# Layer two's third projection begun ahead of the context's norm in bank G0, and the decay logarithms of four token tiles one projection later

## What is computed

```python
h_lat = modulate(rmsnorm(x, g_mix_pre[i]), ...)
h_ctx = modulate(rmsnorm(xc, g_mix_pre[i]), ...)
p = h @ w_in
k, v, lr_f, lr_b = jnp.split(p_state, STATE_SPLITS, axis=-1)
logg_f = jax.nn.log_sigmoid((lr_f @ w_dec_f + b_dec_f)) / GLA_TAU
logg_b = jax.nn.log_sigmoid((lr_b @ w_dec_b + b_dec_b)) / GLA_TAU
```

## Time and profile before

| | |
|---|---|
| median of 3 runs | 1609.02 us (1607.54 to 1609.69) |
| the profiled execution, its own time | 1608.07 us |
| its span, first to last instruction | 1606.3 us |
| mean granted TensorE clock in the span | 0.988 of full speed |
| busy: PE, VectorE, ScalarE, POOL | 1542.8, 861.7, 568.2, 592.9 us |

### The profile page before, as it was taken

The page is one execution under the profiler, slowest core; times in us unless marked ns, Lnnn a source line. Parts: engine busy times, 40 slices in busy tenths (PEclk is TensorE's granted clock), DMA queues, the critical chain, the costliest instruction groups (busy, mean ns, idle before and its releaser), DMA issues.

```text
span 1606.3 us, 22916 instructions
## 1 busy us (share of the span) xinstructions
PE 1542.8 (96%) x9056; PEld 1388.5 (86%) x9056; DVE 861.7 (54%) x1316; ACT 568.2 (35%) x916; POOL 592.9 (37%) x309
## 2 busy tenths in 40 slices
PE   5999999999999999999999989999999999999997
PEld 2899999886899999999998769888898888888887
DVE  1576888536756326661465675477656332322237
ACT  4644214425444214441243255432525321231221
POOL 0532211245325524653255223332152544444441
PEclk9999999999999999999999999999999999999999
DMA  9544431355322212222122341653040333322321
GB/s 370 199 166 153 160 123 62 113 172 206 118 63 70 79 37 95 74 72 66 53 80 91 119 158 53 209 198 105 28 158 27 107 106 128 128 94 92 104 82 63
DMA packets 54062, 183.93 MB, mean 115 GB/s; under 512 B 5650, under 2 KB 10642, under 8 KB 51028
## 3 DMA queue, kind: packets, MB, share of 16 engines
q1 hardware_dynamic: 47826, 168.85, 30.9%
q10 hardware_dynamic: 6146, 13.83, 2.5%
HBM read 171.13 MB, written 11.53 MB: 114 GB/s over the span
## 4 chain that ended last, share of the span: by engine, by line
PE 89%; DVE 3%; ACT 3%; DMA 2%; POOL 1%; issue 1%; SPq 1%; DVEq 0%; ACTq 0%; POOLq 0%
PE A L1022 61%; PE A L1274 8%; PE N L1274 4%; PE G L1274 4%; PE G L1329 1%; PE A L1208 1%; PE A L1202 1%; PE G L1177 1%; DMA raw<-modw 1%; PE G L1136 1%; DMA raw<-stream 1%; PE A L1170 1%; PE N L1190 1%; PE A L1216 1%; PE N L1120 1%
## 5 line engine op out<-in xcount | busy, mean ns | idle before, releaser
L960 POOL TENSOR_TENSOR w_lo<-raw,w_hi 128x1024 fp32r<-128x1024 f32 (+2 forms) x163 | 385.7, 2368 | 659.7 <-ACT w_hi L1356 622.5
L1022 PE MATMUL A<-h_hi,w_hi 128*128 128x512 f32 (+2 forms) x1264 | 416.3, 360 | 22.5 <-POOL h_lo L1005 10.4
L1022 PE MATMUL A<-h_hi,w_lo 128*128 128x512 f32 (+2 forms) x1264 | 406.2, 352 | 0.0
L1022 PE MATMUL A<-h_lo,w_hi 128*128 128x512 f32 (+2 forms) x1264 | 406.0, 352 | 0.0
L1356 ACT ACTIVATE w_hi<-raw 128x1024 fp32r<-128x1024 f32 (+2 forms) x163 | 167.3, 1028 | 379.2 <-PE A L1022 336.0
L1022 PEld LDWEIGHTS A<-h_hi,w_hi 128*128 128x128 f32 x1264 | 237.1, 192 | 66.1 <-POOL h_lo L1005 16.2
L1022 PEld LDWEIGHTS A<-h_hi,w_lo 128*128 128x128 f32 x1264 | 239.0, 192 | 22.0
L1022 PEld LDWEIGHTS A<-h_lo,w_hi 128*128 128x128 f32 x1264 | 239.4, 192 | 21.1 <-issue 0.5
L1022 PE MATMUL A<-g_hi,w_hi 128*128 128x384 f32 (+2 forms) x480 | 146.2, 347 | 3.8 <-DVE g_lo L1847 2.0
L1022 PE MATMUL A<-g_lo,w_hi 128*128 128x384 f32 (+2 forms) x480 | 145.2, 345 | 0.0
L1022 PE MATMUL A<-g_hi,w_lo 128*128 128x384 f32 (+2 forms) x480 | 145.0, 345 | 0.0
(11 more groups left out here) (313 smaller groups left out, 2648.2 us busy)
## 6 DMA issues: line engine op xcount, KB each, us to landing
raw<-stream SPq DMA_DIRECT2D x150, 512.0 KB, 3.7
mraw<-modv SPq DMA_DIRECT2D x54, 512.0 KB, 4.3
mraw<-modw SPq DMA_DIRECT2D x10, 1024.0 KB, 6.4
raw<-pairs SPq DMA_DIRECT2D x18, 512.0 KB, 4.8
raw<-modw SPq DMA_DIRECT2D x6, 1024.0 KB, 14.7
x<-x_keep ACTq DMA_DIRECT2D x4, 1536.0 KB, 13.5
raw<-stream SPq DMA_DIRECT2D x16, 384.0 KB, 3.1
bg<-modv SPq DMA_DIRECT2D x10, 512.0 KB, 4.1
```

The source lines that it names most:

```text
L960: pool.tensor_tensor(lo, like_chunk(n, raw[:, n % RAW, 0:WIDTH[n]]), hi.bitcast(F32), ALU.subtract).then_inc(lo_done, 1)
L1022: m = pe.matmul(dst[:, at:at + t1 - t0], a, b[:, k, t0:t1], start=(first and p == 0), stop=(last and p == 2))
```

## The change

Six edits belong together.

1. In the hand-over to layer two, three entries `pre` do the latent half of projection 2 (512 columns) into G0, for the feature tiles 0 and 1, 2 to 4, and 5 to 7 (`PRE`). The first stands ahead of the eight `sq` entries, the second behind the fourth, the third behind the eighth, ahead of the norm.
2. Projection 2 of layer two then does the context's 256 columns alone.
3. ScalarE copies the latent half from G0 to `kT` behind its copies of lr, and the context half from the A bank in the place of the old copy.
4. In layer two the three pairs of `z` stand behind projections 1, 3 and 4, not 1, 2 and 3. Layer one keeps its order.
5. Layer two's z begin with G1, not with G0.
6. Layer two's dot products move by one projection (5 to 19, not 4 to 18).

```diff
--- before.py
+++ after.py
@@ -20,6 +20,7 @@
 HEADS, DK, DV, RANK, CHUNK = 4, 64, 128, 16, 64
 HID = 2816 // P
 BLOCKS = (8, 8, 6)
+PRE = ((0, 2), (2, 5), (5, KT))
 EPS = 1e-6
 LN_SET = "natural_log_exp_and_others"
 
@@ -43,7 +44,7 @@
 
 GROUPS, MW = 3, 2048
 DOTS = {0: dict([(x, 3) for x in range(4, 6)] + [(x, 2) for x in range(6, 19)]),
-        1: dict([(x, 2) for x in range(4, 13)] + [(x, 1) for x in range(13, 19)])}
+        1: dict([(x, 2) for x in range(5, 14)] + [(x, 1) for x in range(14, 20)])}
 FFN_DOTS = {("ffn_in", 0): 3, ("ffn_out", 0): 3, ("ffn_in", 1): 2}
 SLOTS = 3
 X_PIECES = 2
@@ -173,8 +174,14 @@
             piece(6)
             steps("res", 1, range(KT))
             order.append(("head", L, w, 1, 0))
-            steps("sq", 1, range(KT))
             if w:
+                order.append(("pre", L + 1, 0))
+            steps("sq", 1, range(4))
+            if w:
+                order.append(("pre", L + 1, 1))
+            steps("sq", 1, range(4, KT))
+            if w:
+                order.append(("pre", L + 1, 2))
                 order.append(("keep", 1, 1))
             order.append(("rstd",) + nxt + (1,))
             steps("nrm", 1, range(KT))
@@ -232,7 +239,7 @@
         m = list(range(2 * KT, 6 * KT))
         for x, (name, j, _) in enumerate(W_IN):
             order.append(("proj", L, x))
-            if 1 <= x <= 3:
+            if x in ((1, 3, 4) if L else (1, 2, 3)):
                 order.append(("z", L, z.pop(0)))
                 order.append(("z", L, z.pop(0)))
             if 4 <= x <= 9:
@@ -355,7 +362,7 @@
 
 
 FOUR_UNITS = ("N1", "N0", "G0", "G1")
-FULL = ("z", "turn", "suffix", "dstate", "four", "gate", "score", "o", "msq", "mean")
+FULL = ("pre", "z", "turn", "suffix", "dstate", "four", "gate", "score", "o", "msq", "mean")
 
 
 class Plan:
@@ -384,8 +391,10 @@
                 elif kind == "four":
                     units = [FOUR_UNITS[tiles_of(L).index(e[2]) % 4]]
                 else:
-                    units = [f"G{g % 2}"]
+                    units = [f"G{(g + L) % 2}"]
                     g += 1
+            elif kind == "pre" and e[2] == 0:
+                units = ["G0"]
             elif kind == "suffix":
                 units = ["N1"]
             elif kind == "dstate":
@@ -1068,7 +1077,16 @@
                         continue
                     unit_free(e)
                     lo_wait(pe, n0)
-                    project(A[PLAN.acc[e]], n0, in_banks(tokens(L, name)), H).then_inc(chunk_used, 1)
+                    ranges = [(SEQ, TOK, SEQ)] if e[1:] == (1, 2) else in_banks(tokens(L, name))
+                    project(A[PLAN.acc[e]], n0, ranges, H).then_inc(chunk_used, 1)
+                elif kind == "pre":
+                    n, ks = PLAN.n0[("proj", L, 2)], range(*PRE[e[2]])
+                    unit_free(e)
+                    lo_wait(pe, n)
+                    for k in ks:
+                        h_wait(pe, L, 0, 0, k)
+                        m = split_matmul(G[0], n, [(0, SEQ, 0)], k, H, k == 0, k == KT - 1)
+                    m.then_inc(full["pre"], 1)
                 elif kind == "head":
                     w, j, s = e[2:]
                     to = ("ffn_in", L, 0, 0) if w == 0 else ("proj", L + 1, j)
@@ -1476,13 +1494,18 @@
                         half = lambda t, r: t[64 * r:64 * r + 32, 0:T].rearrange("p (a c t) -> p c a t", c=2, t=P)[:, r, :, :]
                         act.activation(half(lrT, 0), half(src, 0), ACT.Copy)
                         act.activation(half(lrT, 1), half(src, 1), ACT.Copy).then_inc(free[f"A{PLAN.acc[e]}"], 1)
+                        if L:
+                            act.wait_ge(full["pre"], len(PRE))
+                            act.activation(kT[:, 1, 0:SEQ], G[0][:, 0:SEQ], ACT.Copy).then_inc(free["G0"], 1)
                         high(n0 + RING)
                         act.preload_act_table_set(LN_SET)
                         continue
                     dst = {"k": kT[:, j % 2, 0:T], "v": (vst if j < 2 else cgz)[:, j % 2, 0:T], "q": qT[:, j % 2, 0:T],
                            "f": uF[:, j % 2, 0:T], "c": cgz[:, j % 2, 0:T], "b": bg[:, j % 2, 0:T], "r": r_s[:, j, 0:T]}[name]
                     src = src[:, 0:T]
-                    if e[2] > 1:
+                    if e[1:] == (1, 2):
+                        dst, src = kT[:, 1, SEQ:TOK], A[PLAN.acc[e]][:, SEQ:TOK]
+                    elif e[2] > 1:
                         dst, src = by_bank(dst, T), out_banks(PLAN.acc[e], T)
                     if name == "r":
                         m = act.activation(dst, src, ACT.Silu)
```

## The result

The changed kernel takes 1617.62 us (median of 5 runs, 1615.02 to 1619.65); the kernel before took 1608.97 us beside it. The ratio is 1.0055 (95% interval 1.0044 to 1.0067): slower by 8.65 us, where +7.46 was forecast and the range reached from 1612.5 to 1620.0. The profiled execution took 1619.65 us, the longest of the five, in a span of 1617.9.

What follows compares the result with a forecast made beforehand. TensorE (PE) was taken as the bound, busy 1542.8 us and 89% of the last chain. 3.54 - 5.58 + 7.00 + 2.5 = +7.46 us on 1609.02 gave 1616.5 us, range 1612.5 to 1620.0.

Steps and rivals of the forecast that it cites:

- The forecast's own range: 1615.4 to 1617.9 us, from slow clock of 1.6 to 3.35 us and 0.2 us on the wait at the transposes.
- norm delayed by 15 matmuls: Hand-over to layer two: six matmuls ahead of the first sum and nine after the fourth delay the context's norm, +3.54 us.
- projection 2 shrinks: Layer two's third projection: 8.53 us of matmuls become 2.95 us in the old place, -5.58 us.
- pause at the transposes: Ahead of the kT transposes: PE stands until VectorE has last read both z results of the last pair, +7.00 us.
- slow clock behind it: On the transposes and projection 5: PE runs at 1.2 GHz after the long pause, +2.5 us, between 1.6 and 3.35.
- slow clock under the context heads: Context heads after the norm: no loss to the lower clock in the forecast, 1.7 us in the rival with chance 0.16.
- rival 1: Context heads also run at the slower clock, costing 1.7 us more: +9.2 us, 1618.2 us; chance 0.16.
- the likeliest case: The forecast itself: +7.46 us, 1616.5 us, with the pause ahead of the kT transposes; chance 0.62.
- rival 2: Filling the norm's pause removes a slow stretch under the context heads, giving back 1.9 us: +5.6 us, 1614.6; chance 0.10.
- the wait at 966.95: Kernel before, context head: PE waited for POOL's low parts until 966.95, so the slow stretch there was taken to cost nothing.
- Part one's gain: Matmuls moved ahead in the hand-over: 3.54 - 5.58 = -2.04 us, so projection 3 begins earlier.
- Rivals 3, 4 and 5: Short wait at transposes, 1607.0 us (0.04); moved work held up, 1618.5 (0.03); half the pause given back, 1613.0 (0.05).

Runs made afterwards that it cites:

- both measurements: The changed kernel, unedited, measured twice: first 1617.62 us, ratio 1.0055, then again beside later runs 1613.70 us, ratio 1.0035.
- the last z in N: The changed kernel with layer two's last two z (token tiles 4 and 5) in banks N0 and N1: 1606.27 us, ratio 0.9984; measured again 1607.03 us.
- the z alone: The kernel before with only layer two's z behind projections 1, 3 and 4 and dot products one projection later: 1617.76 us, ratio 1.0054.

## Why the prediction was right

The direction, the place and the main term held; the range from 1612.5 to 1620.0 took in both measurements. The forecast's own range, 1615.4 to 1617.9, took in the first, 1617.62, and not the second, 1613.70. That +7.46 lies so near the first, +8.65, is in part luck: in its trace two misses offset each other, too much slow clock behind the pause and none under the context heads. Step by step (the first measurement's profile, then the second's):

| step | forecast, us | measured, us | from |
|---|---|---|---|
| norm delayed by 15 matmuls | +3.54 | +3.43, +3.46 | the Ln above; first part's start to first z, 954.98 to 974.85, against 16.41 |
| projection 2 shrinks | -5.58 | -5.67 | first to third pair 19.19 less one pair, 1.06, against 12.46 |
| pause at the transposes | +7.00 | +6.91, +6.92 | the rows above |
| slow clock behind it | +2.5 | +1.35, +1.58 | 10.42 and 10.65 to the next transposes, against 9.07 with the last z in N |
| slow clock under the context heads | 0 (rival 1: 1.7) | +2.1, 0 | 20.62 and 18.51, first sum to first z |
| sum | +7.46 | +8.2, +6.3 | the whole stretch, 62.50 and 60.63 against 54.11: +8.4, +6.5 |

- **The pause** was the likeliest case's core, and the runs bear out its reason: it goes when the banks of the pair change, stays when the parts move, and comes alone with the z.
- **The slow clock behind the pause** was taken too large. The middle of the rows' stretches was taken, 5 us at the lower clock; here it was 2.9 and 3.2 us from the start of the transposes. With the z alone more was lost, 2.0 us by the 11.02 to the next transposes. Why these stretches were shorter than the longer ones of the earlier trace rows stays open; waits inside those do not explain it, since PE is busy for all of the 5.95 us one. The Trainium skill (TensorE: Matmul & The Clock Gate, "Why this matters for your kernels") has pauses send the clock back, and the traces agree at this place in every profile that has the pause: the clock stood at 0.50 to 0.53 behind it in all four.
- **The context heads** were given no slow clock in the forecast, and 0.16 in rival 1. The case was not an either-or: it happens in some executions of one program and not in others. That fits two medians, 1617.62 and 1613.70, on both sides of the forecast, but is not shown to be their cause.
- **The filled pause pays nothing in clock** (rival 2), as the wait at 966.95 had told. With the slow stretch gone, the changed kernel needs 19.87 us from the end of the latent head to the first z, and that is the old 16.41, whose heads ran in the slow stretch, and 3.46, the fifteen matmuls put ahead.
- **Part one's gain**, -2.04 us, came out as the kernel with the last z in N shows it: by the medians -2.72 and -1.39 us against the kernel before, by its two traces -2.05 and -2.04 (52.06 and 52.07 from the end of the latent head to the second transposes, against 54.11).
- Rivals 3, 4 and 5 did not occur: the wait is 6.91 us, the parts start without any wait, and nothing behind gives the pause back (from the second transposes to the span's end 597.8 us, as 597.9 before; all ten profiles lie between 595.9 and 598.1, with the pause or without).
- Two slips of the prediction change nothing. Of the two waits inside the context head of projection 0 the longer is one of 0.76 us at 962.74, not the 0.57 that it shows. And 1617.9, the upper end of the forecast's own range, is 1617.5 by the two terms that it names; it takes the 0.4 us allowed for VectorE's dot products to get there.

## What to carry to other kernels

When a piece of work is taken out from under a chain of another engine, ask what that chain releases, and who stands directly behind it in the new order; a wait that a bank's reader imposes may be removed by another bank rather than another order, as twice here. Work that is to fill a pause belongs behind the last instruction that the pause's chain waits for: ahead of it, it delayed the chain here by its whole length, 3.4 us for fifteen matmuls.

## What was not expected

Matmuls worth 5.5 us fit at no cost into a place where the trace showed one pause of 2.59 us, because the heads behind it had waited in small pieces as well, in part at the lower clock, and then ran nearly in one. And the lower clock comes and goes at unchanged places: 872 to 880 us stood at 0.83 in one profile and at 1.00 in another, 1240 to 1248 us at 0.63 and 1.00. A median of five runs of one kernel moved by 3.9 us between two measurements: the second ratio, 1.0035, lies outside the first's interval, 1.0044 to 1.0067.
